# Parting the turnings of a slab pair, and handing six low parts of each two-pass expert to GpSimd

## The chip, the cores and the metric

The kernel runs on one core of a Trainium2 chip. The metric is the device time of one execution in microseconds (us), lower is better. Engines are named as in the profile: PE (TensorE) with its weight load PEld, DVE (VectorE), ACT (ScalarE), POOL (GpSimd), SP (SyncE, which here only issues loads).

## The reference: what is computed

An encoder trunk of two layers over 256 tokens of width 1024, in fp32. Layer 0 has a pooling mixer and a dense SwiGLU. Layer 1 has a dilated attention mixer and eight SwiGLU experts, of which each token uses two:

```
logits = (h @ router)
top_v, top_i = lax.top_k(logits, 2);  gates = softmax(top_v)
for e in range(8):
    gu = h @ w_gate_up[e]                       # (1024, 2*3584)
    y += gate[..., e] * ((silu(gu[..., :3584]) * gu[..., 3584:]) @ w_down[e])
out = rmsnorm(x)
```

The change touches only the experts of layer 1.

## The kernel before, in words

**Tiles.** All weights come from memory in tiles of 128 x 2048 fp32, 1 MB each. An expert has 42 of them (`FFN_TILES`). I number them 0 to 41 inside their expert: 0 to 23 are three pairs of slabs of gate and up columns (`PAIRS`, eight tiles a pair: four of gate, four of up), 24 to 27 the single seventh slab (`SINGLE`), 28 to 41 the down projection (`DOWN`).

**Split products.** The matmuls run on fp32r operands, so each fp32 weight tile is split into a high and a low part. For tile t, SP loads `raw[t % 7]`. ACT writes the high part `whi[t % 3]` (`make_hi`, L333). DVE subtracts it from the raw tile and writes the low part `wlo[t % 3]` (`make_lo`, L339): a subtraction of two tiles in SBUF, written to SBUF. PE then multiplies. `make_hi` and `make_lo` of tile t wait until PE has finished tile t-3 (`tile_used`), since there are three slots (`CUT`). SP reloads a `raw` slot when the low part made from it is done (`RAW` = 7 slots).

**Two kinds of expert.** Items 0, 2, 4, 6 are full experts of up to 128 tokens (`full_item`): three passes of the weights, 12 matmuls of 512 columns a tile. Items 1, 3, 5, 7 are two-pass experts of up to 64 tokens (`half_item`): the high and the low part of 64 tokens stand side by side in 128 columns, so that a tile takes two passes, 8 matmuls (L940 on the high part, L941 on the low part). The two kinds alternate.

**Turnings.** After a pair of slabs g-1 is complete, PE turns its two slabs (`turn(j)`), so that they can serve as stationary operand of the down projection. In a two-pass expert a turning is 16 small matmuls (L954), which also fold the two halves. Before the change both turnings of a pair stand together behind tile 8g+1, and for the third pair behind tile 25. The seventh slab is turned behind tile 30. On turned slabs ACT does `slab_silu`, DVE `slab_mul` (L1874), ACT `slab_hi`, DVE `slab_lo` (L1439).

**Order.** Each engine's program is written out by hand. `ahead(t)` of ACT or DVE makes the part of tile t+3, and the small operations stand between such calls. The waits are on counting semaphores: `hi_done` for high parts, `lo_done` for low parts. GpSimd gathers the tokens of an expert and scatters its results by indirect DMA (L511, L519), and has no other work in the experts.

Of the kernel before, what the change touches and what calls it, by code (L numbers as in the profile page):

```python
# [28 lines left out]
P = 128  # L29
RAW = 7  # L30
CUT = 3
# [6 lines left out]
SLABS = FF // 512  # L38
# [3 lines left out]
E = 8  # L42
CAP = 128
HALF_CAP = 64
LOW = 4
# [6 lines left out]
ALU = mybir.AluOpType  # L52
ACT = mybir.ActivationFunctionType
F32 = mybir.dt.float32
# [11 lines left out]
FFN_TILES = DOWN + 2 * DT  # L66
# [9 lines left out]
def count(i, per, plus=0):  # L76

    if isinstance(i, int):
        return i * per + plus
    register, step, first = i  # L80
    return register * (step * per) + (first * per + plus)


def one(i):
# [7 lines left out]
def encoder(nc, x_in, rel_bias, gains_t, norm_ffn, norm_final, a_w_in, a_w_group, a_scale, a_w_out,  # L92
            b_w_in, b_w_out, f_w_gate_up, f_w_down, m_router, m_w_gate_up, m_w_down,
            c_ident, c_pool, c_bucket, c_band, c_class, c_tri, c_iota, c_tab, c_dump, out):
    with ExitStack() as ctx:
# [133 lines left out]
        spare_zero = sem("spare_zero")  # L229
        c_in = [sem(f"const{i}") for i in range(15)]  # L230
        raw_full = [sem(f"raw_full{i}") for i in range(RAW)]
        hi_done, lo_done, tile_used = sem("hi_done"), sem("lo_done"), sem("tile_used")
# [96 lines left out]
        def make_hi(act, t, item=0):  # L329
# [2 lines left out]
                act.wait_ge(tile_used, count(item, FFN_TILES, t - CUT + 1))  # L332
            nc.scalar.activation(whi[:, t % CUT], raw[:, t % RAW], ACT.Copy).then_inc(hi_done, 1)  # L333

        def make_lo(dve, t, item=0):
            dve.wait_ge(hi_done, count(item, FFN_TILES, t + 1))
            if t >= CUT:
                dve.wait_ge(tile_used, count(item, FFN_TILES, t - CUT + 1))
            nc.vector.tensor_tensor(wlo[:, t % CUT], raw[:, t % RAW], whi[:, t % CUT].bitcast(F32),  # L339
                                    ALU.subtract).then_inc(lo_done, 1)  # L340
# [33 lines left out]
        def _(sp):  # L374
# [20 lines left out]
            def load_expert(t, n, e, by_half=False):  # L395

                t_all = T_MOE + t
                if t >= FFN_TILES:
                    t -= FFN_TILES
                sp.wait_ge(lo_done, count(n, FFN_TILES, t_all - RAW + 1))  # L400
# [66 lines left out]
        def _(pool):  # L467
# [36 lines left out]
                pool.dma_start(acc_dram[r * P:r * P + P, :], x[:, r % NT]).then_inc(acc_done, 16)  # L504

            pool.wait_ge(hn_out, 32)
            summed = 48
            for n in range(E - 1):
                pool.wait_ge(from_ready, n + 1)
                rows = slice(0, HALF_CAP if n % 2 == 0 else P)  # L510
                nc.gpsimd.indirect_dma_start(e_tok[rows], None, hn_dram,  # L511
                                             bass.IndirectOffsetOnAxis(from_rows[rows, 0:1], 0)).then_inc(e_full, 16)
                pool.wait_ge(slot_ready, n + 1)
                pool.wait_ge(y_hi, 2 * n + 2)
                width = P if n % 2 == 0 else HALF_CAP
                for first in range(0, P, width):
                    pool.wait_ge(acc_done, summed)
                    to = slice(first, first + width)
                    nc.gpsimd.indirect_dma_start(acc_dram, bass.IndirectOffsetOnAxis(to_rows[0:width, 0:1], 0), y_out[to],  # L519
                                                 None, compute_op=ALU.add).then_inc(acc_done, 16)  # L520
                    summed += 16
            pool.wait_ge(acc_done, summed)
            for tb in range(NT):
                pool.dma_start(x[:, tb], acc_dram[tb * P:tb * P + P, :]).then_inc(x_back, 16)

            pool.wait_ge(x_final, 1)
            pool.wait_ge(c_in[C_GAIN4], 16)
# [3 lines left out]
        @block.tensor  # L531
        def _(pe):
            def tile_ready(t, item=0):
                pe.wait_ge(lo_done, count(item, FFN_TILES, t + 1))

            def turn_x(n, kh):

# [344 lines left out]
            def full_item(n, k, amid=lambda g: None, late=lambda: None, before_down=lambda: None):  # L882
# [20 lines left out]
                for g in range(PAIRS):  # L903
                    if g >= 1:
                        pe.wait_ge(silu_done, count(k, SLABS, PAIRS0 + 2 * g))
                    for q in range(4):
                        if g == 0 and q == 2:
                            third_wait(n)
                        product(8 * g + q, eTh, eTl, (G, S0))
                        if g >= 1 and q == 1:  # L910
                            turn(2 * g - 2)
                            turn(2 * g - 1)
                    amid(g)
                    for q in range(4):
                        product(8 * g + 4 + q, eTh, eTl, (U, S1))
# [1 line left out]
                product(SINGLE, eTh, eTl, (G,))  # L917
                product(SINGLE + 1, eTh, eTl, (G,))
                turn(2 * PAIRS - 2)
                turn(2 * PAIRS - 1)  # L920
                amid(PAIRS)
                product(SINGLE + 2, eTh, eTl, (U,))
                product(SINGLE + 3, eTh, eTl, (U,))
                before_down()
                for qn in range(2 * DT):
# [7 lines left out]
            def half_item(n, k, amid=lambda g: None, late=lambda: None, by_half=False, before_down=lambda: None):  # L933
# [25 lines left out]
                for g in range(PAIRS):  # L959
                    if g >= 1:  # L960
                        pe.wait_ge(gate_copied, count(k, SLABS, 2 * g))
                    for q in range(4):
                        if g == 0 and q == 2:
                            third_wait(n)
                        product(8 * g + q, eTh, (G, S0))
                        if g >= 1 and q == 1:
                            turn(2 * g - 2)
                            turn(2 * g - 1)
# [7 lines left out]
                turn(2 * PAIRS - 1)  # L976
                amid(PAIRS)
                product(SINGLE + 2, eTh, (U,))
                product(SINGLE + 3, eTh, (U,))
                before_down()  # L980
                for t in range(DOWN, FFN_TILES):
# [61 lines left out]
        def _(act):  # L1043
# [211 lines left out]
            def full_item(n, k, y_cut, late=lambda: None, alone=False, amid=lambda g: None):  # L1255
# [15 lines left out]
                for g in range(PAIRS):  # L1271
                    t, a, b = 8 * g, 2 * g, 2 * g + 1
                    ahead(t, t + 1, t + 2)
                    if g >= 1:
                        hidden_hi(a - 2)
                    ahead(t + 3)
                    if g >= 1:
                        hidden_hi(a - 1)
                    amid(g)
                    silu(a)  # L1280
# [6 lines left out]
                ahead(SINGLE + 2)  # L1287
                hidden_hi(SLABS - 2)
                ahead(SINGLE + 3)
# [8 lines left out]
            def half_item(n, k, y_cut, late=lambda: None, by_half=False, amid=lambda g: None):  # L1298
# [25 lines left out]
                for g in range(PAIRS):  # L1324
                    t, a, b = 8 * g, 2 * g, 2 * g + 1
                    ahead(t, t + 1, t + 2)
                    if g >= 1:
                        slab_silu(a - 2)
                    ahead(t + 3)
                    if g >= 1:  # L1330
                        slab_silu(a - 1)
                    amid(g)
                    copy_gate(a)
                    ahead(t + 4)
                    if g >= 1:
                        slab_hi(a - 2)
                    copy_gate(b)
                    ahead(t + 5)
                    if g >= 1:
                        slab_hi(a - 1)  # L1340
                    ahead(t + 6, t + 7)
                    copy_up(a)
                    copy_up(b)
                ahead(SINGLE, SINGLE + 1)
                copy_gate(SLABS - 1)
                slab_silu(SLABS - 3)
                ahead(SINGLE + 2)
                slab_silu(SLABS - 2)
                ahead(SINGLE + 3)
                copy_up(SLABS - 1)  # L1350
                slab_hi(SLABS - 3)
                ahead(DOWN)
                slab_hi(SLABS - 2)
# [64 lines left out]
        def _(dve):  # L1418
# [400 lines left out]
            def full_item(n, k, amid=lambda t: None, late=lambda: None, y_cut=lambda h: None, alone=False):  # L1819
# [18 lines left out]
                for g in range(PAIRS):  # L1838
                    t, a, b = 8 * g, 2 * g, 2 * g + 1
                    ahead(t, t + 1, t + 2)  # L1840
                    if g >= 1:
                        hidden_lo(a - 2)
                    ahead(t + 3)
                    if g >= 1:
                        hidden_lo(a - 1)
                    ahead(t + 4, t + 5, t + 6, t + 7)
                    mul(a)
                    mul(b)
                ahead(SINGLE, SINGLE + 1)
                hidden_lo(SLABS - 3)  # L1850
                ahead(SINGLE + 2)
                hidden_lo(SLABS - 2)
                ahead(SINGLE + 3)
# [9 lines left out]
            def half_item(n, k, amid=lambda t: None, late=lambda: None, y_cut=lambda h: None, by_half=False):  # L1863
# [34 lines left out]
                ahead(SINGLE + 2)  # L1898
                slab_mul(SLABS - 3)
                ahead(SINGLE + 3)  # L1900
                slab_mul(SLABS - 2)
                slab_lo(SLABS - 3)
                ahead(DOWN)
                slab_lo(SLABS - 2)
                if by_half:
# [121 lines left out]
```

## Time and profile before

| | |
|---|---|
| time, median of 3 runs | 1575.45 us (1574.39 to 1576.29) |
| the profiled execution | time 1576.29 us, span 1574.4 us |
| busy share PE, DVE, ACT, POOL | 95%, 74%, 64%, 8% |
| granted PE clock, mean | 0.994 of full speed |
| a full expert, from scatter to scatter | 122.8 us |
| a two-pass expert, likewise | 110.2 us |

Times in timelines are us from the start of the span. A row of a timeline has the start, the duration, engine, line, operation, tiles and shape, how many instructions it merges (x4), and in brackets how long the engine stood idle before it and whose end released it. Two instructions of an engine that run back to back overlap a little in the records: low parts of DVE of 2.29 us start 2.20 us apart.

### The profile page before, as it was taken

What the parts mean: (1) busy time and instruction counts of PE and PEld (TensorE: products, weight loads), DVE (VectorE), ACT (ScalarE), POOL (GpSimd) and SP (SyncE); (2) the same over time, 40 slices, a digit from 0 to 9 for tenths busy, and PEclk for the clock granted to TensorE, in tenths of its full rate; (3) what the DMA queues carried; (4) which work ended last, traced back from release to release, by engine and by line L of the source; (5) the groups of instructions that cost most, each with busy time, mean ns of one, the idle gap of its engine ahead of it and who ended that gap; (6) DMA issues with size and microseconds to landing.
All of it is one profiled execution on the core that took longest, in us unless ns stands there. A gap on an engine that the chain in (4) does not pass through costs nothing.

```text
span 1574.4 us, 19686 instructions
## 1 busy us (share of the span) xinstructions
PE 1498.0 (95%) x7570; PEld 1212.3 (77%) x7570; DVE 1169.5 (74%) x1009; ACT 1001.0 (64%) x861; POOL 127.6 (8%) x130
## 2 busy tenths in 40 slices
PE   8999999999999989999998999999999989999995
PEld 6888888899879977787676887677887677887674
DVE  4555544464565466998889898889898989898987
ACT  5443443343453356776878776878777877777875
POOL 0000000032215032200000000000000000000000
PEclk9999999999999999999999999999999999999998
DMA  9655555566426622999999999999999999999994
GB/s 333 219 166 187 187 171 180 191 208 214 161 69 211 212 99 80 384 377 362 377 409 398 399 375 361 388 407 396 399 350 382 387 406 393 404 369 359 396 388 149
DMA packets 151123, 468.34 MB, mean 297 GB/s; under 512 B 9792, under 2 KB 15936, under 8 KB 138480
## 3 DMA queue, kind: packets, MB, share of 16 engines
q1 hardware_dynamic: 144720, 453.93, 78.1%
q0 software_dynamic: 2816, 9.96, 2.3%
q10 hardware_dynamic: 3488, 3.13, 0.6%
q8 instruction: 62, 1.02, 0.3%
q14 instruction: 37, 0.30, 0.1%
HBM read 459.62 MB, written 7.37 MB: 297 GB/s over the span
## 4 chain that ended last, share of the span: by engine, by line
PE 77%; DVE 12%; ACT 5%; issue 4%; DMA 1%; SPq 0%; DVEq 0%; ACTq 0%
DVE wlo L339 9%; PE bS L358 6%; PE bS L357 6%; PE bS L356 6%; PE bY L356 6%; PE bY L358 6%; PE bY L357 6%; ACT whi L333 4%; PE bG L356 4%; PE bU L356 4%; PE bU L358 4%; PE bG L358 4%; PE bU L357 4%; PE bG L357 4%; PE bT L954 2%
## 5 line engine op out<-in xcount | busy, mean ns | idle before, releaser
L339 DVE TENSOR_TENSOR wlo<-raw,whi 128x2048 fp32r<-128x2048 f32 x426 | 969.5, 2295 | 320.9 <-ACT whi L333 317.5
L333 ACT ACTIVATE whi<-raw 128x2048 fp32r<-128x2048 f32 x426 | 813.1, 1914 | 461.8 <-PE bS L358 207.0
L940 PE MATMUL bY<-whi,hTh 128*128 128x512 f32 x224 | 93.2, 416 | 10.3 <-DVE wlo L339 9.5
L941 PE MATMUL bY<-wlo,hTh 128*128 128x512 f32 x224 | 89.9, 401 | 0.0
L356 PE MATMUL bY<-whi,hTh 128*128 128x512 f32 x224 | 89.7, 400 | 0.0
L357 PE MATMUL bY<-whi,hTl 128*128 128x512 f32 x224 | 88.9, 397 | 0.0
L358 PE MATMUL bY<-wlo,hTh 128*128 128x512 f32 x224 | 88.9, 397 | 0.0
L941 PE MATMUL bS<-wlo,eTh 128*128 128x512 f32 x192 | 76.3, 397 | 0.0
L940 PE MATMUL bS<-whi,eTh 128*128 128x512 f32 x192 | 76.2, 397 | 0.0
L356 PE MATMUL bS<-whi,eTh 128*128 128x512 f32 x192 | 76.1, 396 | 0.0
L357 PE MATMUL bS<-whi,eTl 128*128 128x512 f32 x192 | 76.1, 396 | 0.0
L358 PE MATMUL bS<-wlo,eTh 128*128 128x512 f32 x192 | 76.1, 396 | 0.0
L482 POOL TENSOR_TENSOR bias<-biasrev,band 128x256 f32<-128x256 f32 x32 | 29.9, 933 | 506.8 <-DMA biasrev<-toeplitz 382.3
L940 PE MATMUL bU<-whi,eTh 128*128 128x512 f32 x128 | 55.4, 433 | 14.4 <-DVE wlo L339 13.7
L940 PEld LDWEIGHTS bY<-whi,hTh 128*128 128x128 f32 x224 | 42.7, 190 | 32.5 <-issue 21.1
L940 PE MATMUL bG<-whi,eTh 128*128 128x512 f32 x128 | 54.5, 426 | 13.4 <-DVE wlo L339 13.3
L356 PE MATMUL bG<-whi,eTh 128*128 128x512 f32 x128 | 51.7, 404 | 3.5 <-DVE eTl L1439 3.5
L356 PE MATMUL bU<-whi,eTh 128*128 128x512 f32 x128 | 51.4, 402 | 1.0 <-DVE wlo L339 1.0
L940 PEld LDWEIGHTS bU<-whi,eTh 128*128 128x128 f32 x128 | 24.0, 188 | 35.5 <-DVE wlo L339 31.5
L941 PE MATMUL bU<-wlo,eTh 128*128 128x512 f32 x128 | 50.9, 397 | 0.0
L941 PE MATMUL bG<-wlo,eTh 128*128 128x512 f32 x128 | 50.9, 397 | 0.0
L357 PE MATMUL bU<-whi,eTl 128*128 128x512 f32 x128 | 50.8, 397 | 0.0
(458 smaller groups left out, 3170.9 us busy)
## 6 DMA issues: line engine op xcount, KB each, us to landing
raw<-in_m_w_gate_up_dram SPq DMA_DIRECT2D x224, 1024.0 KB, 9.3
raw<-in_m_w_down_dram SPq DMA_DIRECT2D x112, 1024.0 KB, 7.1
raw<-in_b_w_in_dram SPq DMA_DIRECT2D x36, 1024.0 KB, 5.1
raw<-in_f_w_gate_up_dram SPq DMA_DIRECT2D x28, 1024.0 KB, 5.1
raw<-in_f_w_down_dram SPq DMA_DIRECT2D x14, 1024.0 KB, 5.0
raw<-in_a_w_out_dram SPq DMA_DIRECT2D x4, 1024.0 KB, 15.6
biasrev<-toeplitz SPq DMA_DIRECT2D x32, 128.0 KB, 4.8
raw<-in_b_w_out_dram SPq DMA_DIRECT2D x4, 1024.0 KB, 5.0
```

The lines of the kernel that those rows point to most:

```text
L333: nc.scalar.activation(whi[:, t % CUT], raw[:, t % RAW], ACT.Copy).then_inc(hi_done, 1)
L339: nc.vector.tensor_tensor(wlo[:, t % CUT], raw[:, t % RAW], whi[:, t % CUT].bitcast(F32), ALU.subtract).then_inc(lo_done, 1)
L356: pe.matmul(dst, a[0], b[0], start=start, stop=False)
L357: pe.matmul(dst, a[1], b[0], start=False, stop=False)
L358: return pe.matmul(dst, a[0], b[1], start=False, stop=stop)
L482: nc.gpsimd.tensor_tensor(to[:, 0:S].rearrange("p (a m) -> p a m", a=4), rev(0, 4), band[:, qt].rearrange("p (a m) -> p a m", a=4), ALU.add)
L940: pe.matmul(backward(banks[s], 0, 512), xs[:, kb], w[0], start=kb == 0, stop=False)
L941: mm = pe.matmul(backward(banks[s], 0, 512), xs[:, kb], w[1], start=False, stop=stop)
L954: mm = pe.matmul(bank[:, to], hidden_block(rows, c, by_half), fold[:], start=True, stop=True)
```

## The change

1. In every two-pass expert GpSimd makes the low parts of tiles 6, 12, 18, 24, 29 and 34 (`POOL_LOWS`, `make_lo_pool`); DVE skips them. They have a semaphore of their own, `lo_pool`. `low_ready` picks the semaphore for PE (`tile_ready`) and for SP's reloads. That is 24 low parts of 336.
2. The second turning of a pair moves one tile down, for both kinds of expert: `turn(2g-2)` stays behind tile 8g+1, `turn(2g-1)` goes behind tile 8g+2; for the third pair `turn(5)` goes behind tile 26.
3. On ACT and DVE some small operations move by one tile to fit.

```diff
+POOL_LOWS = (6, 12, 18, 24, 29, 34)
+def by_pool(t, n):
+    u = t - T_MOE
+    if not isinstance(n, int) or u < 0:
+        return False
+    n, u = n + u // FFN_TILES, u % FFN_TILES
+    return n % 2 == 1 and n < E and u in POOL_LOWS
...
+        def low_ready(engine, t, item=0):
+            engine.wait_ge(lo_pool if by_pool(t, item) else lo_done, lows(t, item))
+
+        def make_lo_pool(pool, t, item):
+            pool.wait_ge(hi_done, item * FFN_TILES + t + 1)
+            pool.wait_ge(tile_used, item * FFN_TILES + t - CUT + 1)
+            nc.gpsimd.tensor_tensor(wlo[:, t % CUT], raw[:, t % RAW], whi[:, t % CUT].bitcast(F32),
+                                    ALU.subtract).then_inc(lo_pool, 1)
+
         def make_lo(dve, t, item=0):
+            if by_pool(t, item):
+                return
...
             for n in range(E - 1):
+                lows_of(n, POOL_LOWS[:4])
+                rows = slice(0, HALF_CAP if n % 2 == 0 else P)
                 pool.wait_ge(from_ready, n + 1)
                 nc.gpsimd.indirect_dma_start(e_tok[rows], None, hn_dram,
...
+                lows_of(n, POOL_LOWS[4:])
...
+            lows_of(E - 1, POOL_LOWS[:2])
             pool.wait_ge(acc_done, summed)
...
+            lows_of(E - 1, POOL_LOWS[2:])
...
                         product(8 * g + q, eTh, (G, S0))
-                        if g >= 1 and q == 1:
-                            turn(2 * g - 2)
-                            turn(2 * g - 1)
+                        if g >= 1 and q in (1, 2):
+                            turn(2 * g - 3 + q)
...
                 turn(2 * PAIRS - 2)
-                turn(2 * PAIRS - 1)
                 amid(PAIRS)
                 product(SINGLE + 2, eTh, (U,))
+                turn(2 * PAIRS - 1)
                 product(SINGLE + 3, eTh, (U,))
...
@@ ACT, half_item
-                    ahead(t + 6, t + 7)
+                    ahead(t + 6)
                     copy_up(a)
+                    ahead(t + 7)
                     copy_up(b)
```

On GpSimd, from the scatter of item 0 to the first scatter of item 1, the queue reads as follows before (L511 is the gather of the next tokens into `e_tok`, L519 the scatter-add of `y_out`):

```order
L519 DMA summed<-y_out,to_rows 384x1024 [waits acc_done,y_hi,slot_ready]
L511 DMA e_tok<-normed,from_rows 128x1024 [waits from_ready]
L519 DMA summed<-y_out,to_rows 384x1024 [waits acc_done,y_hi,slot_ready]
L519 DMA summed<-y_out,to_rows 384x1024 [waits acc_done]
L511 DMA e_tok<-normed,from_rows 64x1024 [waits from_ready]
```

In the changed kernel, with its own line numbers (L368 is the new low part):

```order
L564 DMA summed<-y_out,to_rows 384x1024 [waits acc_done,y_hi,slot_ready]
L368 TENSOR_TENSOR wlo<-raw,whi 128x2048 [waits tile_used,hi_done] x4
L555 DMA e_tok<-normed,from_rows 128x1024 [waits from_ready]
L368 TENSOR_TENSOR wlo<-raw,whi 128x2048 [waits tile_used,hi_done] x2
L564 DMA summed<-y_out,to_rows 384x1024 [waits acc_done,y_hi,slot_ready]
L564 DMA summed<-y_out,to_rows 384x1024 [waits acc_done]
```

Four low parts stand in front of the gather of the next item's tokens, and two between the gather and the scatter.

On PE, at the third pair of the first two-pass expert (tile 17, the turnings of slabs 2 and 3, tile 18), the program before:

```order
L940 MATMUL bS<-whi,eTh 128x512
L941 MATMUL bS<-wlo,eTh 128x512
L954 MATMUL bT<-fold,mbuf 128x64 [waits jt_mul,up_copied,gate_copied]
L954 MATMUL bT<-fold,mbuf 128x64 x7
L954 MATMUL bX<-fold,mbuf_odd 128x64 [waits jt_mul,up_copied,gate_copied]
L954 MATMUL bX<-fold,mbuf_odd 128x64 x7
L940 MATMUL bG<-whi,eTh 128x512 [waits lo_done]
L941 MATMUL bG<-wlo,eTh 128x512
```

The changed kernel at the same place (eight matmuls of tile 18 now stand between the two turnings, and they wait for GpSimd):

```order
L1000 MATMUL bT<-fold,mbuf 128x64 [waits jt_mul,up_copied,gate_copied]
L1000 MATMUL bT<-fold,mbuf 128x64 x7
L986 MATMUL bG<-whi,eTh 128x512 [waits lo_pool]
L987 MATMUL bG<-wlo,eTh 128x512
L986 MATMUL bG<-whi,eTh 128x512
L987 MATMUL bG<-wlo,eTh 128x512
L986 MATMUL bS<-whi,eTh 128x512
L987 MATMUL bS<-wlo,eTh 128x512
L986 MATMUL bS<-whi,eTh 128x512
L987 MATMUL bS<-wlo,eTh 128x512
L1000 MATMUL bX<-fold,mbuf_odd 128x64 [waits jt_mul,up_copied,gate_copied]
L1000 MATMUL bX<-fold,mbuf_odd 128x64 x7
```

The second turning moved behind tile 18; the number of instructions on PE is the same.

## Rows read from the trace of the kernel before

**Rows 1.** The page: busy times, and the rate of all transfers in 40 slices

```profile
PE 1498.0 (95%) x7570; PEld 1212.3 (77%) x7570; DVE 1169.5 (74%) x1009; ACT 1001.0 (64%) x861; POOL 127.6 (8%) x130
...
GB/s 333 219 166 187 187 171 180 191 208 214 161 69 211 212 99 80 384 377 362 377 409 398 399 375 361 388 407 396 399 350 382 387 406 393 404 369 359 396 388 149
```

**Rows 2.** Windows of one full and two two-pass experts (items 2, 3, 7)

```profile
core 0: us, PE busy (x) PEld busy (x) DVE busy (x) ACT busy (x) POOL busy (x), PEclk, DMA share, GB/s
863.50:986.30 122.80, 122.67 (x545) 98.82 (x543) 106.03 (x66) 89.17 (x61) 5.83 (x4) 1.00 1.00 379
986.30:1096.30 110.00, 99.29 (x457) 75.14 (x458) 99.08 (x66) 90.50 (x75) 2.90 (x3) 1.00 1.02 397
...
1452.00:1562.00 110.00, 97.81 (x442) 73.39 (x442) 94.36 (x58) 84.99 (x71) 3.04 (x3) 0.98 0.90 338
```

**Rows 3.** Waits in the two-pass expert of item 1 (753.3 to 863.5): total, times, longest

```profile
DVE wlo L339 <- ACT whi L333: 11.4, 8, 3.4
...
PE bU L940 <- DVE wlo L339: 3.7, 8, 0.8
PE bG L940 <- DVE wlo L339: 3.4, 7, 0.8
```

**Rows 4.** Timeline of DVE in that expert

```profile
754.38 18.07 DVE L339 TENSOR_TENSOR wlo<-raw,whi 128x2048 fp32r<-128x2048 f32 x8 [0.66 <-ACT whi L333]
772.76 4.49 DVE L339 TENSOR_TENSOR wlo<-raw,whi 128x2048 fp32r<-128x2048 f32 x2 [0.31 <-ACT whi L333]
780.13 2.29 DVE L339 TENSOR_TENSOR wlo<-raw,whi 128x2048 fp32r<-128x2048 f32 x1 [2.88 <-ACT whi L333]
782.34 0.42 DVE L1874 TENSOR_TENSOR th<-bT,tsilu 128x256 f32<-128x256 f32 x1
782.67 2.28 DVE L339 TENSOR_TENSOR wlo<-raw,whi 128x2048 fp32r<-128x2048 f32 x1
...
790.28 8.90 DVE L339 TENSOR_TENSOR wlo<-raw,whi 128x2048 fp32r<-128x2048 f32 x4
...
804.99 2.28 DVE L339 TENSOR_TENSOR wlo<-raw,whi 128x2048 fp32r<-128x2048 f32 x1
...
827.93 2.28 DVE L339 TENSOR_TENSOR wlo<-raw,whi 128x2048 fp32r<-128x2048 f32 x1
...
840.80 4.48 DVE L339 TENSOR_TENSOR wlo<-raw,whi 128x2048 fp32r<-128x2048 f32 x2
```

**Rows 5.** Timeline of PE in that expert

```profile
772.30 1.99 PE L954 MATMUL bT<-fold,mbuf 128*128 128x64 f32 x16
774.12 2.05 PE L954 MATMUL bX<-fold,mbuf_odd 128*128 128x64 f32 x16
...
792.62 0.51 PE L940 MATMUL bG<-whi,eTh 128*128 128x512 f32 x1 [0.34 <-DVE wlo L339]
794.62 1.99 PE L954 MATMUL bT<-fold,mbuf 128*128 128x64 f32 x16
...
815.33 0.50 PE L940 MATMUL bG<-whi,eTh 128*128 128x512 f32 x1 [0.34 <-DVE wlo L339]
```

**Rows 6.** Timeline of ACT in that expert (high parts of tiles 13 and 34)

```profile
778.19 1.91 ACT L333 ACTIVATE whi<-raw 128x2048 fp32r<-128x2048 f32 x1 [3.66 <-PE bS L941]
...
836.31 1.92 ACT L333 ACTIVATE whi<-raw 128x2048 fp32r<-128x2048 f32 x1 [1.71 <-PE bY L941]
```

**Rows 7.** Timeline, POOL's longest two-input operations, and DVE beside the last

```profile
610.01 2.38 POOL L494 TENSOR_TENSOR hn<-x,gain 128x1024 f32<-128x1024 f32 x1 [26.34 <-DVE x L1458]
...
1562.97 2.35 POOL L528 TENSOR_TENSOR hn<-x,gain 128x1024 f32<-128x1024 f32 x1 [99.31 <-DVE x L1962]
...
1563.58 2.82 DVE L1429 CUSTOM_DVE_ANT_0 squares<-x 128x1024 f32<-128x1024 f32 x1
```

**Rows 8.** Timeline of the attention, DVE and POOL side by side

```profile
346.32 3.02 DVE L339 TENSOR_TENSOR wlo<-raw,whi 128x2048 fp32r<-128x2048 f32 x1 [0.59 <-ACT whi L333]
...
346.34 0.84 POOL L482 TENSOR_TENSOR bias<-biasrev,band 128x256 f32<-128x256 f32 x1
...
347.14 2.57 POOL L485 TENSOR_TENSOR bias<-biasrev,classes 128x128 f32<-128x128 f32 x1
```

**Rows 9.** Two lines as wholes: duration in ns, min/median/max

```profile
L485 POOL TENSOR_TENSOR bias<-biasrev,classes x64: 507/525/2587, 343.6 to 583.1; 128x128 f32<-128x128 f32 x64
...
L1429 DVE CUSTOM_DVE_ANT_0 hn<-x x3: 1215/1218/1221, 23.6 to 326.0; 128x1024 f32<-128x1024 f32 x3
```

More of the change, by code:

```diff
@@ L81, in count, with lows @@
     return register * (step * per) + (first * per + plus)
+POOL_LOWS = (6, 12, 18, 24, 29, 34)
[5 more added lines that the diff above has]
+    return n % 2 == 1 and n < E and u in POOL_LOWS
+def lows(t, n):
+    if not isinstance(n, int):
+        return count(n, FFN_TILES, t + 1 - LOW * len(POOL_LOWS))
+    all_tiles = n * FFN_TILES + t + 1
+    u = all_tiles - 1 - T_MOE
+    if u < 0:
+        return all_tiles
+    n, u = divmod(u, FFN_TILES)
+    if by_pool(t=T_MOE + u, n=n):
+        return len(POOL_LOWS) * (n // 2) + POOL_LOWS.index(u) + 1
+    here = sum(p < u for p in POOL_LOWS) if n % 2 == 1 and n < E else 0
+    return all_tiles - len(POOL_LOWS) * (min(n, E) // 2) - here
 def one(i):
@@ L231, in encoder @@
         raw_full = [sem(f"raw_full{i}") for i in range(RAW)]
-        hi_done, lo_done, tile_used = sem("hi_done"), sem("lo_done"), sem("tile_used")
+        hi_done, lo_done, lo_pool, tile_used = sem("hi_done"), sem("lo_done"), sem("lo_pool"), sem("tile_used")
         chain = sem("chain")
@@ L399, in load_expert @@
                     t -= FFN_TILES
-                sp.wait_ge(lo_done, count(n, FFN_TILES, t_all - RAW + 1))
+                low_ready(sp, t_all - RAW, n)
                 gu, dn = m_w_gate_up[0, one(e)], m_w_down[0, one(e)]
@@ L506, in _, with lows_of @@
             pool.wait_ge(hn_out, 32)
+            def lows_of(n, tiles):
+                if n % 2 == 1:
+                    for t in tiles:
+                        make_lo_pool(pool, T_MOE + t, n)
             summed = 48
             for n in range(E - 1):
+                lows_of(n, POOL_LOWS[:4])
+                rows = slice(0, HALF_CAP if n % 2 == 0 else P)
                 pool.wait_ge(from_ready, n + 1)
-                rows = slice(0, HALF_CAP if n % 2 == 0 else P)
                 nc.gpsimd.indirect_dma_start(e_tok[rows], None, hn_dram,
                                              bass.IndirectOffsetOnAxis(from_rows[rows, 0:1], 0)).then_inc(e_full, 16)
+                lows_of(n, POOL_LOWS[4:])
                 pool.wait_ge(slot_ready, n + 1)
@@ L533, in tile_ready @@
             def tile_ready(t, item=0):
-                pe.wait_ge(lo_done, count(item, FFN_TILES, t + 1))
+                low_ready(pe, t, item)
             def turn_x(n, kh):
@@ L965, in half_item @@
                         product(8 * g + q, eTh, (G, S0))
-                        if g >= 1 and q == 1:
-                            turn(2 * g - 2)
-                            turn(2 * g - 1)
+                        if g >= 1 and q in (1, 2):
+                            turn(2 * g - 3 + q)
                     amid(g)
@@ L975, in half_item @@
                 turn(2 * PAIRS - 2)
-                turn(2 * PAIRS - 1)
                 amid(PAIRS)
                 product(SINGLE + 2, eTh, (U,))
+                turn(2 * PAIRS - 1)
                 product(SINGLE + 3, eTh, (U,))
@@ L1276, in full_item @@
                     ahead(t + 3)
+                    amid(g)
+                    silu(a)
                     if g >= 1:
                         hidden_hi(a - 1)
-                    amid(g)
-                    silu(a)
                     ahead(t + 4)
@@ L1286, in full_item @@
                 hidden_hi(SLABS - 3)
-                ahead(SINGLE + 2)
+                ahead(SINGLE + 2, SINGLE + 3)
                 hidden_hi(SLABS - 2)
-                ahead(SINGLE + 3)
                 ahead(DOWN, DOWN + 1, DOWN + 2, DOWN + 3, DOWN + 4)
@@ L1345, in half_item @@
                 copy_gate(SLABS - 1)
+                ahead(SINGLE + 2)
                 slab_silu(SLABS - 3)
-                ahead(SINGLE + 2)
-                slab_silu(SLABS - 2)
                 ahead(SINGLE + 3)
                 copy_up(SLABS - 1)
+                slab_silu(SLABS - 2)
                 slab_hi(SLABS - 3)
@@ L1842, in full_item @@
                         hidden_lo(a - 2)
-                    ahead(t + 3)
+                    ahead(t + 3, t + 4)
                     if g >= 1:
                         hidden_lo(a - 1)
-                    ahead(t + 4, t + 5, t + 6, t + 7)
+                    ahead(t + 5, t + 6)
                     mul(a)
+                    ahead(t + 7)
                     mul(b)
@@ L1850, in full_item @@
                 hidden_lo(SLABS - 3)
-                ahead(SINGLE + 2)
+                ahead(SINGLE + 2, SINGLE + 3)
                 hidden_lo(SLABS - 2)
-                ahead(SINGLE + 3)
                 mul(SLABS - 1)
@@ L1900, in half_item @@
                 ahead(SINGLE + 3)
+                slab_lo(SLABS - 3)
                 slab_mul(SLABS - 2)
-                slab_lo(SLABS - 3)
                 ahead(DOWN)
```

## The prediction

> **What bounds the kernel now.** I read the busy shares first: PE is busy 95% of the span, DVE 74% [rows 1]. Such a mean mixes stages, so I next cut the experts into windows [rows 2]. A full expert takes 122.8 us and PE is busy for 122.7 of them: PE bounds it, and nothing that only relieves DVE can shorten it. A two-pass expert takes 110.0 us, with PE busy 99.3 and DVE 99.1. There no engine is full, so I read the waits [rows 3]. PE waits for low parts of DVE again and again, 0.5 us at a time; DVE waits only 11.4 us, in 8 pieces, for high parts of ACT.
>
> The timeline of DVE says why [rows 4]. From 754.38 it makes eight low parts (tiles 3 to 10) in 18.07 us, nearly back to back at its pitch of 2.20 us. A tile costs PE only 2.0 us (792.62 to 794.62) [rows 5], so PE waits for DVE. After the low part of tile 12 DVE stands 2.88 us, until 780.13. The reason is on PE [rows 5]: two turnings of 1.82 us each (772.30, then 774.12) keep it from freeing a slot of the ring of three, and ACT, which needs that slot, waits 3.66 us until 778.19 [rows 6]. The same shape recurs at the other two pairs. So a two-pass expert is DVE's subtractions in series, plus three stalls behind turnings. Both sides are tight: PE 2.0 us, ACT 1.94, DVE 2.3 and the handovers make some 6.5 us for the round of three slots, and three pitches of DVE make 6.6.
>
> **What a low part costs on GpSimd.** No row has this shape. The nearest are its two-input operations of 128x1024: 2.38 and 2.35 us [rows 7]. Twice that is 4.7 us, the upper end. From 128x256 in 0.84 us [rows 8] to 128x1024 in 2.35 is 1.97 ns an element; 1024 elements more make 4.37, the lower end. I take 4.5. The Trainium skill's GPSIMD Engine Reference, section Performance versus the Vector engine, gives 4.497 us for a two-input fp32 operation of 2048 elements. By that figure the sum below would stay as it is.
>
> **Whether it runs beside DVE.** This decides the case, and the attention stage shows it. At 346.34 GpSimd begins an operation of 0.84 us; the low part that DVE issues at 346.32 takes 3.02 us instead of 2.29, as if it had begun when GpSimd ended [rows 4, 8]. GpSimd's next operation, issued at 347.14, takes 2.57 us instead of its median 0.525: it waits for DVE to end [rows 8, 9]. At the end of the kernel DVE's L1429, which reads x twice, takes 2.82 us instead of 1.22; GpSimd's operation beside it ends at 1565.32, and 1563.58 + 2.82 - 1.22 = 1565.18 [rows 7, 9]. So two operations that each read two tiles in SBUF exclude each other, long ones too, from start to about 0.1 us before the recorded end. The held time is then about 4.4 us against DVE's 2.2.
>
> The Trainium skill says the same in SBUF — State Buffer, section Who interferes with whom, but for the whole instruction: the second to issue is blocked until the first ends. With 4.5 instead of 4.4 us held, the sum would be some 2 us longer.
>
> **The sum, for a two-pass expert.** T is when PE starts the tile in front of the first turning; the frame is: tile 2.0 us until its waiter starts (792.62 to 794.62), turning 1.85, high part 1.94 until DVE starts (778.19 to 780.13) [rows 4 to 6].
>
> *Tile 6.* The rows of tiles 3 to 10 run without a gap worth naming and the ring is as tight as DVE, so the high part of 6 is there when DVE ends tile 5, and that of 7 is not yet. GpSimd gets its turn at once, and DVE is shut out until it ends. Tiles 6 and 7 need 4.4 + 2.2 instead of 2.2 + 2.2: +2.2 us. PE waits for it, since it was waiting already; nothing hides it.
>
> *Tiles 12 to 14.* Before, T = 770.3 and the low part of tile 14 starts at T+12.4 (782.67). Parted turnings let PE finish tile 10 at T+2.0+1.85+2.0 = T+5.85 and tile 11 at T+9.7, so the high part of 14 is there at T+11.8. GpSimd has tile 12 from T+4.7 to T+9.1; tile 13 follows on DVE to T+11.4, the small multiply takes 0.35, and tile 14 starts at T+11.8. Here the six-tenths gained by the parting are kept, and the low part costs nothing, since it lies in the old stall: -0.6.
>
> *Tiles 18 to 22.* Tile 18 stands between the two turnings. T = 792.62. Its low part on GpSimd is done at T+4.5, while PE could start it at T+3.85. PE ends it at T+6.5, turns, ends tile 19 at T+10.4, and the low part of 22 can start at T+12.4. Before it was T+12.4 (804.99): 0.
>
> *Tile 24.* As tile 6, with no stall near: +2.2. A small DVE operation that reads two SBUF tiles is shut out with it.
>
> *Tiles 29, 30.* T = 815.33. The high part of 29 is ready at T+8.2, 0.4 for the index matmuls included; GpSimd holds until T+12.6, and the low part of 30 starts at T+12.7 against T+12.6 before (827.93): +0.1.
>
> *Tile 34.* The high part is made from 836.31 [rows 6] and ready at 838.3; GpSimd holds until 842.7; DVE's next low part began at 840.80: +1.9. DVE's multiply runs meanwhile, but is too short to matter.
>
> Together 2.2 - 0.6 + 0 + 2.2 + 0.1 + 1.9 = **+5.8 us**, times four experts +23 us. A second way agrees: DVE and GpSimd together need 99.1 + 6 x 2.2 = 112.3 us, less 0.7 of overlap, plus some 3 us of idle that stays (0.66 at the start, 1.3 before tile 29, the rest in pieces): 114.6 to 115, so +4.6 to +5. I keep the first, which follows the order.
>
> **Edits at nothing.** Full experts: PE is full (122.7 of 122.8), the turnings keep their number, and no operation moved on ACT or DVE comes later than PE needs it, since DVE has 16 us free. Cover gone, they would show as waits of PE. The gather of tokens stands behind four low parts but still before that of tile 29; it is wanted by PE only behind tile 38. SP's reload of six slots comes up to 2.5 us later; seven slots with several loads under way cover that. The moved copy of ACT delays one high part per pair by 0.5 us in front of the turning stall, which takes it up.
>
> From the profiled execution, 1576.3 + 23 = 1599; it lies 0.8 us above the median, so from the median 1575.45 + 23 = **1598 us**. With 4.2 us held instead of 4.4 the expert costs 5.0 (1595), with 4.7 about 7.5 (1605).
>
> **Rivals.**
> - *No exclusion in long operations, or GpSimd yields.* For: all collisions before have GpSimd operations no longer than 2.4 us. DVE would be rid of 13.2 us an expert, but the ring of three still has to wait 4.5 us for the part itself: tiles 6, 24 and 34 would come 2 us late and be caught up only in part at the next turning. I work out 0 to +1 us an expert: 1575 to 1580. Chance 0.06.
> - *The other side: parting pays and GpSimd is hidden.* Parting alone gives 0.6 at each of three pairs. If the low parts of 6, 24 and 34 fell into waits, for instance because DVE gets ahead between them, three parts of 0.6 on four experts are 7 us: 1568. It decides where a low part costs less than 0.3 us on average. Against: DVE has no idle time around 6 and 24 [rows 4]. Chance 0.06. No gain can be large anyway: the transfers already run at 397 GB/s in a two-pass expert against a best slice of 409 [rows 1, 2].
> - *GpSimd is slower than I think,* because it writes fp32r, which no row of it shows. By the short rows alone (0.84 us for 256) 2048 elements take up to 6.7 us. At 5.5 us each part costs 1 us more, 24 us in all: 1622. Chance 0.1.
> - *As forecast,* 1590 to 1607: 0.78.
>
> **Numbers.** The run-to-run spread makes 0.2%, 3 us, about what can be told from no change. Faster by more: 0.06. Within: 0.05, most of the first rival. Slower: 0.89. The range for 8 in 10 takes the forecast's own 1590 to 1607 and reaches part way to both sides: 1586 to 1616.
>
> **What would show it.** GpSimd: 24 operations of about 4.5 us. DVE: the low part behind each of them recorded at 3 to 5 us, since it is issued and blocked. PE: one wait of about 2.3 us at tiles 6, 24 and 34, in place of 0.3. DVE's stalls behind turnings nearly gone. Two-pass experts at 115 to 116 us, full ones unchanged at 122.8. I am wrong if DVE's low parts beside GpSimd stay at 2.29 us, or if GpSimd's take over 5 us.

## The result and the profile after

The changed kernel takes 1609.35 us in the median of 4 runs (1608.1 to 1613.11) against 1575.64 before: the ratio is 1.022 (95% interval 1.020 to 1.024), 33.7 us slower. The profiled execution has a span of 1606.9 us against 1574.4. The forecast was 1598, with 1586 to 1616 as the range.

The page of the changed kernel, its parts on busy time, and of its groups the low parts of both makers (L377 is DVE's, L368 GpSimd's):

```profile
PE 1506.0 (94%) x7570; PEld 1223.5 (76%) x7570; DVE 1172.7 (73%) x985; ACT 1002.0 (62%) x861; POOL 239.7 (15%) x154
...
L377 DVE TENSOR_TENSOR wlo<-raw,whi 128x2048 fp32r<-128x2048 f32 x402 | 953.0, 2383 | 340.4 <-ACT whi L360 336.7
...
L368 POOL TENSOR_TENSOR wlo<-raw,whi 128x2048 fp32r<-128x2048 f32 x24 | 112.2, 4673 | 223.3 <-ACT whi L360 223.3
```

GpSimd took 24 low parts from DVE, 24 x 2.29 = 55 us of work, and DVE's busy time did not fall: 1172.7 us against 1169.5 [rows 1]. What left it in number came back in length, since a blocked operation counts as busy. GpSimd's part takes 4.67 us in the mean.

Windows of the first two-pass expert, the full one behind it and the next two-pass one, from scatter to scatter (start:end, length, then busy time of PE, PEld, DVE, ACT, POOL, and PE's granted clock, share and rate of transfers):

```profile
754.65:872.67 118.02, 100.54 (x457) 77.60 (x458) 99.36 (x60) 90.52 (x75) 30.82 (x8) 0.97 0.99 371
872.67:995.45 122.78, 122.66 (x545) 98.84 (x543) 106.20 (x66) 89.21 (x61) 5.80 (x4) 1.00 1.00 378
995.45:1114.14 118.69, 102.59 (x457) 79.07 (x458) 100.38 (x60) 90.76 (x75) 30.90 (x8) 0.96 0.98 369
```

The full expert is unchanged at 122.8 us [rows 2]. The two-pass experts went from 110.2, 110.0, 110.2 and 111.0 us to 118.0, 118.7, 118.4 and 117.5: 31.2 of the span's 32.5 us. The other 1.3 us arise before the first two-pass expert. New is the column of the clock, 0.97 and 0.96 where it was 1.00.

The timeline of DVE in the first of these experts:

```profile
764.79 6.67 DVE L377 TENSOR_TENSOR wlo<-raw,whi 128x2048 fp32r<-128x2048 f32 x2 [2.39 <-ACT whi L360]
772.67 6.90 DVE L377 TENSOR_TENSOR wlo<-raw,whi 128x2048 fp32r<-128x2048 f32 x3 [1.22 <-ACT whi L360]
...
786.72 2.29 DVE L377 TENSOR_TENSOR wlo<-raw,whi 128x2048 fp32r<-128x2048 f32 x1 [0.25 <-ACT whi L360]
...
809.09 2.29 DVE L377 TENSOR_TENSOR wlo<-raw,whi 128x2048 fp32r<-128x2048 f32 x1 [0.64 <-ACT whi L360]
...
833.47 3.00 DVE L377 TENSOR_TENSOR wlo<-raw,whi 128x2048 fp32r<-128x2048 f32 x1 [3.05 <-ACT whi L360]
...
846.58 6.86 DVE L377 TENSOR_TENSOR wlo<-raw,whi 128x2048 fp32r<-128x2048 f32 x2 [1.38 <-ACT whi L360]
```

The first row is tiles 7 and 8: two operations that usually take 4.5 us together took 6.67, since the first was shut out by GpSimd's part of tile 6. Set against [rows 4], and less the 1.3 us by which the expert starts later, the low part of tile 14 starts 2.7 us late (786.72 against 782.67), that of 22 is 2.8 late (809.09 against 804.99), that of 30 ends 4.9 late (836.47 against 830.21), that of 36 ends 6.8 late (853.44 against 845.28), and the expert ends 7.8 late. My sum had 1.6, 1.6, 3.9, 5.8 and 5.8. The steps from tile 14 to 36 agree within 0.2 us; missing are 1.1 us by tile 14 and 1.0 behind tile 36.

What PE did at tile 6 shows what is missing. The timeline of PE in the changed kernel, then the same stretch as a window:

```profile
767.15 0.80 PE L986 MATMUL bU<-whi,eTh 128*128 128x512 f32 x1 [2.54 <-POOL wlo L368]
...
768.17 0.63 PE L986 MATMUL bU<-whi,eTh 128*128 128x512 f32 x1
768.60 0.63 PE L987 MATMUL bU<-wlo,eTh 128*128 128x512 f32 x1
...
771.41 0.40 PE L986 MATMUL bS<-whi,eTh 128*128 128x512 f32 x1
771.65 0.40 PE L987 MATMUL bS<-wlo,eTh 128*128 128x512 f32 x1
```

```profile
767.00:770.40 3.40, 3.25 (x8) 2.63 (x9) 3.40 (x2) 0.04 (x1) 0.10 (x1) 0.54 1.03 419
770.40:773.80 3.40, 3.40 (x16) 2.67 (x16) 2.18 (x2) 3.08 (x3) 0.00 (x0) 1.00 1.03 410
```

PE waited 2.54 us for GpSimd and then ran at its lower clock, 1.2 GHz: a matmul every 0.43 us instead of every 0.24, eight in 3.4 us instead of sixteen. Tile 6 took PE 3.3 us (767.15 to 770.46) instead of 2.0, and gave back its slot 1.3 us later for that. The Trainium skill, TensorE: Matmul & The Clock Gate, section HAM oscillation, warns of this: idle gaps between bursts of matmuls send the clock back to half, and each burst then begins slow. The trace agrees in kind; the gaps of the page's example are waits of some 3 to 5 us, and here one of 2.54 us was followed by the lower clock.

### The profile page after: what moved, and what is told of

Read it like the earlier page. It is cut to its first block and busy times, and to the rows that moved or that the text cites. A ratio compares the mean times of both kernels' runs of the same rounds, so it can differ in the third digit from the quotient of the medians.

```text
span 1606.9 us, 19688 instructions
## 1 busy us (share of the span) xinstructions
PE 1506.0 (94%) x7570; PEld 1223.5 (76%) x7570; DVE 1172.7 (73%) x985; ACT 1002.0 (62%) x861; POOL 239.7 (15%) x154
## 5 line engine op out<-in xcount | busy, mean ns | idle before, releaser
L377 DVE TENSOR_TENSOR wlo<-raw,whi 128x2048 fp32r<-128x2048 f32 x402 | 953.0, 2383 | 340.4 <-ACT whi L360 336.7
L368 POOL TENSOR_TENSOR wlo<-raw,whi 128x2048 fp32r<-128x2048 f32 x24 | 112.2, 4673 | 223.3 <-ACT whi L360 223.3
L986 PE MATMUL bG<-whi,eTh 128*128 128x512 f32 x128 | 57.2, 447 | 23.8 <-POOL wlo L368 12.8
L986 PE MATMUL bU<-whi,eTh 128*128 128x512 f32 x128 | 56.5, 441 | 19.2 <-POOL wlo L368 9.6
L564 POOL DMA_INDIRECT summed<-y_out,to_rows x10 | 21.5, 2147 | 272.3 <-issue 253.7
L986 PEld LDWEIGHTS bG<-whi,eTh 128*128 128x128 f32 x128 | 25.7, 201 | 39.9 <-issue 21.3
L394 PE MATMUL bG<-whi,eTh 128*128 128x512 f32 x128 | 52.4, 409 | 3.6 <-DVE eTl L1484 3.6
```

The costliest lines, as they stand in the source:

```text
L368: nc.gpsimd.tensor_tensor(wlo[:, t % CUT], raw[:, t % RAW], whi[:, t % CUT].bitcast(F32), ALU.subtract).then_inc(lo_pool, 1)
L394: pe.matmul(dst, a[0], b[0], start=start, stop=False)
L986: pe.matmul(backward(banks[s], 0, 512), xs[:, kb], w[0], start=kb == 0, stop=False)
```

## The experiments

Every run has its own runs of the kernel before beside it (medians 1575.46 to 1575.86). An experiment that changes `POOL_LOWS` also picks the tiles in front of a gather by their number. Theory A was mine after the result: exclusion between DVE and GpSimd, the ring of three, and the clock.

### The parts of the change: which one costs?

```diff
 e1_parting_alone:  POOL_LOWS = ()
 e2_lows_alone:     the kernel before + POOL_LOWS and all that serves them; turnings together
 e3_far_lows:       POOL_LOWS = (6, 24, 34)
 e4_near_lows:      POOL_LOWS = (12, 18, 29)
```

e1_parting_alone. 

> The change without any low part on GpSimd (an empty list of tiles), so only the parted turnings and the moved small operations. Theory A (the parting gives 0.5 to 0.7 us at each of the three pairs of a two-pass expert; everything lost comes from GpSimd): 1.5 to 2.1 us an expert, 6 to 8 us in all, so about 1568.5 us against 1575.6 before; two-pass experts near 108.4 us, full ones 122.8; no stretch of the experts at half the PE clock. Theory B (the parting itself costs, because PE switches more often between kinds of work and a copy of ACT comes earlier): over 1576 us, with longer waits of PE at tiles 10 to 14.

Measured 1569.13 us, ratio 0.995 (0.994 to 0.997). The two-pass experts take 108.0 to 108.4 us. Theory A holds and theory B falls. Parting the turnings gives 6.3 us; it is a small gain hidden in a change that loses. In the profiled executions the four two-pass experts are 2.0, 1.9, 2.2 and 2.7 us shorter, 8.8 in all; the difference to 6.3 lies before the first of them, where the time varies from run to run (see the account below).

e2_lows_alone. 

> The kernel before with the six low parts on GpSimd, but both turnings of a pair together as before. Theory A: tiles 6, 24 and 34 cost as in the change; tiles 12 and 18 lie in the long stall behind the turnings and cost nothing; tile 29 costs 1.9 us, since it comes out of that stall late. That is 8.2 us an expert and some 2.5 us for stretches at half the PE clock: 1575.6 + 43, about 1618 us. Theory B (the parting costs): below the change's 1609, at 1600 or less.

Measured 1623.75 us, 1.030 (1.029 to 1.032): 48.3 us slower than before, 5 more than expected, and slower than the whole change. Theory B falls here too. The trace shows what the expectation had too low: in the first three two-pass experts PE now waits 3.0 us at tile 29 as well (1.2 to 1.4 in the changed kernel), a stretch at half clock follows there too, and the experts have 14 such stretches of 3.4 us against the change's 10.

e3_far_lows. 

> The change with GpSimd making only tiles 6, 24 and 34, those that have no stall beside them. Theory A: 2.2 + 2.2 + 1.9 us for them, 2.0 to 2.2 us of half clock behind the long waits, less 1.75 us for the parting: 6.6 to 6.9 us an expert, so 1602 to 1603 us. Theory C (the cost is spread over all low parts of GpSimd alike, for instance by its start and its semaphores): half of what the six cost beyond the parting, (1609 - 1568)/2, so 1589 us.

Measured 1602.74 us, 1.017 (1.015 to 1.018), as A has it; C falls.

e4_near_lows. 

> The change with GpSimd making only tiles 12, 18 and 29, those beside the turnings. Theory A: they take back what the parting gives at tiles 18 and 29 and nothing at 12, so -0.7 us an expert: 1572 to 1574 us, with PE waiting under 1.3 us at any of them and no stretch of the experts at half clock. Theory C (all alike): 1589 us.

Measured 1572.33 us, 0.998 (0.997 to 0.999). The three low parts beside the turnings cost 3.2 us in all against e1, the three others 33.6 us (e3 less e1). Together that is 36.8 of the 40.2 us that all six cost. PE waits at most 1.17 us for GpSimd, at tile 29, and no stretch of the experts is at half clock. So the cost lies where there is no stall to hide a late tile; theory C falls.

### What of GpSimd's low part costs: exclusion, lateness or clock?

```diff
 e5_memset
-            nc.gpsimd.tensor_tensor(wlo[:, t % CUT], raw[:, t % RAW], whi[:, t % CUT].bitcast(F32),
-                                    ALU.subtract).then_inc(lo_pool, 1)
+            nc.gpsimd.memset(wlo[:, t % CUT, 0:1536].bitcast(mybir.dt.bfloat16), 0.0)
+            last = nc.gpsimd.memset(wlo[:, t % CUT, 1536:2048].bitcast(mybir.dt.uint8), 0)
+            last.then_inc(lo_pool, 1)
 e6_one_input
+            nc.gpsimd.tensor_scalar(wlo[:, t % CUT], raw[:, t % RAW], 0.0, None, ALU.mult).then_inc(lo_pool, 1)
 e7_warm (and e8_memset_warm: the same with the memsets of e5)
                 def product(t, xs, banks):
+                    if t in (6, 24, 34):
+                        if t > 6:
+                            pe.wait_ge(jt_mul, count(k, SLABS, {24: 4, 34: 6}[t]))
+                        for _ in range(10):
+                            pe.matmul(X[:], eTh[:, 0], eTh[:, 0:4].rearrange("p k s -> p (k s)"), start=True, stop=True)
                     tile_ready(T_MOE + t, n)
 e9_short_memset
+            nc.gpsimd.memset(wlo[:, t % CUT].bitcast(F32), 0.0).then_inc(lo_pool, 1)
```

e5_memset. 

> The change with all six tiles, but GpSimd writes zeros into the low part by two memsets (1536 columns as bf16, 512 as bytes) sized for 4.4 us by the rate of the one memset in the trace (1024 elements in 0.95 us); it reads no SBUF. The low parts of 24 tiles are left out. Theory A (what costs is that two operations which both read two tiles in SBUF exclude each other): DVE's low parts beside GpSimd stay at 2.29 us, and the time is that of the ring alone: 1575 to 1585 us. Theory D (what costs is only that the tile's own part comes 4.5 us after its high part, exclusion or not): as the change, 1605 to 1609 us.

Measured 1600.19 us, 1.016 (1.013 to 1.018). The two memsets took 2.66 + 1.80 us, as long as the subtraction. The line of DVE's low parts in this run, and the same line in the changed kernel (durations in ns, min/median/max):

```profile
L378 DVE TENSOR_TENSOR wlo<-raw,whi x402: 2278/2291/2984, 17.0 to 1578.3; 128x2048 fp32r<-128x2048 f32 x134
```

```profile
L377 DVE TENSOR_TENSOR wlo<-raw,whi x402: 2276/2292/4789, 16.8 to 1586.2; 128x2048 fp32r<-128x2048 f32 x134
```

No low part was shut out in the experts any more (the longest of the line is one of the attention's, 2.98 us), and yet the time is 1600, not 1575 to 1585. Neither theory as I had put it holds: exclusion is real, but taking it away gives back only 9.2 us of the 40.2 that the low parts cost over e1. (The stretches at half clock stay: 8 of them here, 10 in the change.) The timeline of DVE in this run says why:

```profile
764.79 4.57 DVE L378 TENSOR_TENSOR wlo<-raw,whi 128x2048 fp32r<-128x2048 f32 x2 [2.39 <-ACT whi L360]
772.67 6.93 DVE L378 TENSOR_TENSOR wlo<-raw,whi 128x2048 fp32r<-128x2048 f32 x3 [3.30 <-ACT whi L360]
```

DVE ended tile 8 2.1 us earlier than in the changed kernel (769.36 against 771.46), and then waited 3.30 us instead of 1.22, until the very same 772.67. Tile 9 needs the slot of tile 6, and tile 6 is late whoever is shut out.

e6_one_input. 

> The change with all six tiles, but GpSimd multiplies the raw tile by zero into the low part, one SBUF input instead of two. The low parts of 24 tiles are left out. By the two rows of this form at 128x1024 it takes 2.7 us, so 5.4 here when nothing disturbs it, and DVE beside the second of them was shut out for 0.33 us only. Theory A in its narrow form (the exclusion holds only while GpSimd reads, and one input is read quickly): DVE's low parts behind it recorded under 3.5 us; 1590 us, between the memset and the change. Theory A in its wide form (any GpSimd operation that reads SBUF shuts DVE out to its end): DVE at 4 to 7 us, 1620 to 1635 us, since it is longer than the subtraction.

Measured 1631.65 us, 1.034 (1.032 to 1.037), which is the number of the wide form, but not by its mechanism. One such operation and the low part of DVE beside it:

```profile
764.47 5.38 POOL L368 TENSOR_SCALAR wlo<-raw 128x2048 fp32r<-128x2048 f32 x1 [6.00 <-ACT whi L360]
```

```profile
766.69 3.59 DVE L376 TENSOR_TENSOR wlo<-raw,whi 128x2048 fp32r<-128x2048 f32 x1 [2.39 <-ACT whi L360]
```

If DVE's low part took its usual 2.29 us once it had begun, it began at 766.69 + 3.59 - 2.29 = 767.99, 1.9 us before GpSimd ended. None in the run takes over 3.88 us. Shut out it is less than by the subtraction, and the kernel is slower all the same: its tiles come 5.4 instead of 4.6 us after their high part. That points to lateness again, but not to it alone: PE waits 3.1 to 3.9 us at tiles 6, 24 and 34, and the experts have 15 stretches of 3.4 us at half clock against 10. This run does not part the two.

e7_warm. 

> The change, with ten extra matmuls of 512 columns (some 2.4 us, into bank X, which is free there; the result is not used) in front of tiles 6, 24 and 34 of the two-pass experts, so that PE does not idle while GpSimd works. Theory A with the clock (two to three stretches of 3.4 us at half the PE clock per two-pass expert, each behind such a wait, cost 2 us an expert): the stretches go, and the time falls by 6 to 9 us, to 1600 to 1603 us. Theory E (the half clock costs nothing, since DVE bounds anyway): 1609 us.

Measured 1599.22 us, 1.015 (1.013 to 1.017): 10.1 us faster than the changed kernel, although it computes more. The clock's records show no stretch at half speed between 26 and 1586 us. Theory E falls; A's 1600 to 1603 is met but for 0.8 us. The two-pass experts are 115.3 to 115.9 us, 2.1 to 2.9 less than in the changed kernel and the 115 to 116 that the prediction had for them.

e8_memset_warm. 

> The two memsets of 4.46 us in place of GpSimd's subtraction (the low parts of 24 tiles are left out) and the ten extra matmuls in front of tiles 6, 24 and 34: neither exclusion nor half clock is left, only that the tile's own part comes 4.5 us after its high part. Theory F (that latency is itself most of the cost, since in a ring of three tiles the round of PE, ACT and the maker of the low part becomes 2.3 us longer and nothing gives it back): the memset alone, 1600.2, less what the matmuls gave the change (10 us), so 1588 to 1592 us. Theory A as in my prediction's first rival (without exclusion the latency is caught up): 1575 to 1580 us.

Measured 1588.81 us, 1.008 (1.005 to 1.011). Theory F holds. With neither exclusion nor half clock, lateness alone costs 1588.8 - 1569.1 = 19.7 us over the parting. The extra matmuls could have been a cost of their own, but they end before the tile is there. At tile 6 of the first two-pass expert, GpSimd and then PE:

```profile
761.92 2.66 POOL L368 MEMSET wlo<- 128x3072 bf16 x1 [5.97 <-ACT whi L360]
764.51 1.80 POOL L369 MEMSET wlo<- 128x2048 uint8 x1
```

```profile
763.81 2.48 PE L988 MATMUL bX<-eTh 128*128 128x512 f32 x10
766.37 0.50 PE L992 MATMUL bU<-whi,eTh 128*128 128x512 f32 x1
```

PE starts tile 6 at 766.37, 0.06 us after GpSimd ended it (764.51 + 1.80 = 766.31). So it is, within 0.1 us, in eleven of the twelve places; only at tile 34 of the last expert do the matmuls hold PE 0.9 us longer.

e9_short_memset. 

> GpSimd writes zeros by one memset of 2048 fp32 elements, by the rows 1.8 us, in place of its subtraction (the low parts of 24 tiles are left out). DVE is rid of six low parts an expert as in the change, with no exclusion and no longer latency than DVE's own. Theory F: what GpSimd's slowness costs is gone, and the relief of DVE can show: faster than the parting alone (1569.1), but only by what the ring allows (a round of 6.1 us against 6.6): 0.5 us for each low part outside the stalls, 1560 to 1567 us. Theory G (DVE's load is what bounds a two-pass expert, so the relief of 13 us an expert shows mostly): under 1550 us.

Measured 1565.18 us, 0.993 (0.990 to 0.995). The memset took 1.81 us. Theory F holds and G falls. Six low parts an expert, 13 us of DVE's work, taken away for nothing are worth 4 us in all. So DVE's load is not what this kernel is short of.

### What the ring allows

e10_three_apart leaves GpSimd out and moves the second turning further.

```diff
                     for q in range(4):
                         product(8 * g + q, eTh, (G, S0))
-                        if g >= 1 and q in (1, 2):
-                            turn(2 * g - 3 + q)
+                        if g >= 1 and q == 1:
+                            turn(2 * g - 2)
                     amid(g)
                     for q in range(4):
                         product(8 * g + 4 + q, eTh, (U, S1))
+                        if g >= 1 and q == 0:
+                            turn(2 * g - 1)
...
-                turn(2 * PAIRS - 1)
+                if by_half:
+                    turn(2 * PAIRS - 1)
                 product(SINGLE + 3, eTh, (U,))
...
-                    if t == DOWN + (0 if by_half else 2):
+                    if t == DOWN and not by_half:
+                        turn(2 * PAIRS - 1)
+                    if t == DOWN + (0 if by_half else 3):
                         turn(SLABS - 1)
...
```

> No low part on GpSimd; the second turning of the first two pairs behind tile 8g+4 instead of 8g+2, that of the third behind tile 28 and the last slab's behind tile 31 (not in the last expert's down projection), with the small operations of ACT and DVE moved to fit. No computation is left out. By the frame of the prediction, two turnings within one round of the ring stop DVE for 2.4 us, and in two rounds for 0.9 each: the low part of tile 14 starts 1.4 us earlier than with the parting by one, that of tile 16 1.2 us earlier. Three pairs in three experts and two in the last make 13 us: 1556 us, or some 1560 if the transfers, already at 397 GB/s there, cannot follow (then ACT would wait for loads). The rival (each turning alone stops the ring as long as PE works on it, wherever it stands): no change against the parting by one, 1569 us.

Measured 1559.96 us in the median of 6 runs, 0.990 (0.988 to 0.992): 15.9 us faster than before and 9 faster than e1. The frame holds and the rival falls; of the two figures forecast it is the second, 1560. The first three two-pass experts take 104.9, 104.3 and 105.6 us. In the first of them the low part of tile 14 starts 1.2 us earlier than in e1, counted from that of tile 3, and that of tile 16 1.3 us. The fourth expert takes 108.4, no less than in e1. Its waits of ACT say why (in all, times, longest):

```profile
ACT whi L360 <- DMA raw<-in_m_w_down_dram: 6.1, 9, 0.8
...
ACT whi L360 <- DMA raw<-in_m_w_gate_up_dram: 3.8, 11, 0.7
```

There the high parts wait 9.9 us for loads (in e1's fourth expert 2.3, in e10's second two-pass expert none in the list): loads have taken the place of the stalls. Why in this expert and not in the first two, where the transfers ran at 404 GB/s against 368 here, was not tested.

## Why the prediction was right or wrong

**The time and the side** were right: 1609.35 lies in the range and is slower as forecast, though 11 us over the middle.

**What bounds the kernel** was right as to the stages: the three full experts between the two-pass ones unchanged to 0.1 us, all but 1.3 us of the loss in the two-pass ones. The stalls behind turnings, the frame, and the gain of the parting were right too: 0.6 us a pair were summed, e1 measured 6.3 us over twelve pairs, 0.5 each (0.7 by the lengths of the experts in its trace). "DVE's subtractions in series" was only half of it. DVE is tied with the round of the ring: in e9 13 us of subtractions an expert are gone from DVE, and against e1 the first three two-pass experts are 1.1 to 1.3 us shorter, the fourth 0.1.

**What a low part costs on GpSimd** was right: taken as 4.5 us, measured 4.54 alone and 4.67 in the mean.

**"This decides the case", of the exclusion, was wrong.** The exclusion is there, as forecast: twenty of DVE's low parts in the two-pass experts are recorded at 3.0 to 4.8 us, and each of them ends 2.15 us after the low part of GpSimd that shut it out. But the first rival, worked out at 1575 to 1580 us without exclusion, failed. e5 has none and takes 1600 us; e8 has neither exclusion nor half clock and takes 1589. The failed step is "would be caught up only in part at the next turning". I had found the round of the ring (6.5 us) as tight as three pitches of DVE (6.6), and did not carry that into this rival: where PE, ACT and the maker of the low part are tied in a round without slack, a late tile makes its successor in the slot late, even if DVE is idle. How much later than in e1 DVE starts a low part in the first two-pass expert, counted from that of tile 3 (us):

| tile | 9 | 14 | 22 | 28 | 37 |
|---|---|---|---|---|---|
| e8, lateness alone | 1.9 | 1.9 | 2.2 | 3.6 | 5.0 |
| e7, lateness and exclusion | 2.2 | 2.2 | 2.8 | 5.1 | 7.8 |

What tile 6 loses is still lost at tile 14, behind a turning: nothing is caught up. And exclusion and ring hardly add, since whichever comes last sets the start: at tile 6 the exclusion adds 0.3 us to what the ring takes, not 2.2; over the whole expert it adds 2.7. So the sum came out right for a reason that it did not have. Its 5.8 us an expert came from exclusion alone, less what the parting gives, and e7, without the half clock, is 5.7, 5.8, 5.5 and 4.3 us longer than before; but in the first expert 5.0 of the 7.8 us over e1 are lateness. The second way, which adds up DVE's and GpSimd's busy times as if exclusion were all, agreed by the same luck.

**The half clock was missing.** I expected waits of PE of 2.3 us at three tiles and did not ask what PE does after such a wait; the column of the clock stood at 1.00 in all windows of the experts before but the last. The waits came as forecast, 2.3 to 2.9 us at each of the twelve places, and the trace after shows 1.2 GHz behind nine of them, two or three in each two-pass expert (3.4 us each time, once 6.8). e7 takes 10 us off by keeping PE at work: that is most of the 11 us between 1598 and 1609. The sum had this cost at nothing.

**The account** over e1: exclusion 10.4 us (e7 less e8; 9.2 as change less e5), half clock 10.1 (change less e7; 11.4 as e5 less e8), lateness 19.7 (e8 less e1). That these add up to the 40.2 us between e1 and the change says nothing, since each term begins where the last one ends; what can be tested is whether a term comes out the same the other way, and the two ways differ by 1.2 us. By the lengths of the four two-pass experts in the profiled executions the terms are 9.8, 10.0 and 20.3.

1.3 us of the profiled span arose before the first two-pass expert. 0.8 of them stand before the experts begin: the first high part of the experts starts at 597.8 us against 597.0. The clock's records of the changed kernel have a half-speed stretch near 583 us, in the attention, but it is not needed for this: in the twelve profiled executions that high part starts anywhere from 595.9 to 599.9 us, and in e7, which has no such stretch, at 598.1. What makes it vary was not tested. The other 0.5 us lie in the first full expert. From its first high part to its scatter it takes 156.4 us in the two kernels with the turnings together (before and e2) and 156.7 to 157.1 in the ten with the turnings parted, a small cost of the parting that the sum had at nothing; its cause stays open.

**The rival of a free relief** (parting pays and GpSimd is hidden) came true only where the tiles lie beside the turnings, in e4, and gave 3.1 us, less than the parting alone. **The rival of a slow GpSimd** did not come: 4.67 us.

## What to carry to other kernels

An operation given to a slower engine costs its lateness, not its share of the load. Before moving it, add up the round of the buffer ring that it sits in: if the round has no slack, most of the extra duration is lost on every such tile, however idle the relieved engine becomes (here 1.4 to 1.9 of 2.3 us at tiles 6, 24 and 34 in e8). Then look at what the waiting engine does after a wait that is new to it; here a wait of 2.5 us on PE cost 1.3 us more through the clock. And try each part of a combined change alone: here a gain of 6 us was hidden under a loss of 40, and the same idea taken further (e10) gave 16.

## What the runs showed of the hardware

- The wait in front did not alone decide on the clock. Of the twelve waits of 2.3 to 2.9 us in the changed kernel nine were followed by half speed. In the first two-pass expert of the changed kernel the wait of 2.54 us before tile 6 was followed by half speed, and one of 2.69 us before tile 24 was not: the stretch from 819 to 821 has a granted clock of 1.00.
- A low part of DVE that GpSimd's subtraction of two tiles shut out ended 2.15 us behind it in all twenty cases of the changed kernel; DVE's alone takes 2.29 us, so it had begun 0.14 us before GpSimd's recorded end. Its waiting is recorded as busy time.
- GpSimd's memset goes by elements, not bytes: 2048 fp32 took 1.81 us, 2048 bytes 1.80 us, 3072 bf16 2.66 us. It did not shut DVE's subtractions out. The Trainium skill, SBUF — State Buffer, section Who interferes with whom, says that such a DVE operation contends with a GpSimd operation that reads SBUF, not with one that only writes it; e5 agrees.
- A GpSimd operation with one input of 128x2048 (a multiplication by a constant, fp32 in, fp32r out) took 5.4 us, longer than the subtraction with two (4.54), and shut DVE out for less: in all thirteen cases of e6 DVE's low part ended 0.41 to 0.43 us behind it, so at its usual 2.29 us it had begun 1.9 us before GpSimd's end. The same section calls the contention an exclusive lock, and says of DVE's two-port modes that the second operation is blocked for the whole of the first; here the lock was shorter than the operation.
